# The last two value pieces of a short convolution later, their first taps on VectorE, and a thirteenth seven-product group in the convolution's columns

## The reference, cut to what matters

```python
cqkv = h @ w_in[:, C_CQKV:C_CQKV + 3072]            # 256 x 3072: queries, keys, values, 8 heads each
qkv = silu(causal_depthwise_conv(cqkv, d_conv_w))   # 4 taps over the tokens, each channel by itself
q_c, k_c, v_c = split(qkv, 3)                       # q_c and k_c are then l2-normalized per head
```

## Time and profile before

| what | value |
|---|---|
| median of three runs | 1515.25 us |
| the profiled execution's own time | 1515.99 us |
| its span, first to last instruction | 1514.1 us |
| TensorE clock granted, mean | 1.000 of full speed |
| busy: PE, DVE, ACT, POOL | 1509.8, 1138.6, 821.5, 367.0 us |

### The profile page before, as it was taken

One profiled execution on the slowest core, in us unless ns is written; L12 is line 12 of the kernel. 1 busy time (PEld: TensorE's weight loads), 2 busy tenths in 40 slices (PEclk: granted clock), 3 DMA queues, 4 the chain that ended last, 5 costly groups with the idle time before them and its releaser, 6 DMA issues.

```text
span 1514.1 us, 19057 instructions
## 1 busy us (share of the span) xinstructions
PE 1509.8 (100%) x6900; PEld 1249.9 (83%) x6900; DVE 1138.6 (75%) x1712; ACT 821.5 (54%) x1100; POOL 367.0 (24%) x612
## 2 busy tenths in 40 slices
PE   9999999999999999999999999999999999999999
PEld 7888888888888887888878888888888888888887
DVE  6889899847769855576579676676557789988894
ACT  6766656587533444554545545544345656555563
POOL 9040131330230040126420254344400112000101
PEclk9999999999999999999999999999999999999999
DMA  9876677976788775558765787798875667696867
GB/s 288 283 238 218 198 250 209 254 225 195 223 252 267 235 221 165 158 184 271 248 203 167 231 248 205 241 277 241 236 244 158 216 217 221 205 263 210 237 228 187
DMA packets 209070, 341.47 MB, mean 226 GB/s; under 512 B 53161, under 2 KB 60632, under 8 KB 208720
## 3 DMA queue, kind: packets, MB, share of 16 engines
q1 hardware_dynamic: 184784, 288.66, 61.2%
q0 software_dynamic: 24144, 51.57, 13.1%
q10 hardware_dynamic: 48, 0.02, 0.0%
HBM read 312.81 MB, written 30.83 MB: 227 GB/s over the span
## 4 chain that ended last, share of the span: by engine, by line
PE 98%; DVE 1%; ACT 0%; issue 0%; DMA 0%; DVEq 0%
PE acc L1289 25%; PE acc L1292 25%; PE acc L1291 25%; PE mix L1292 2%; PE mix L1291 2%; PE mix L1289 2%; PE mix L1305 2%; PE mix L1307 2%; PE mix L1306 2%; PE acc L1305 2%; PE acc L1307 2%; PE acc L1306 2%; PE mix L1398 1%; PE mix L1481 1%; PE mix L1470 0%; PE mix L1391 0%
## 5 line engine op out<-in xcount | busy, mean ns | idle before, releaser
L2021 DVE TENSOR_TENSOR w_lo<-w_raw,w_hi 128x1024 fp32r<-128x1024 f32 (+1 forms) x503 | 604.0, 1216 | 252.8 <-ACT w_hi L1626 247.9
L1626 ACT ACTIVATE w_hi<-w_raw 128x1024 fp32r<-128x1024 f32 (+1 forms) x503 | 522.5, 1049 | 371.8 <-PE acc L1292 277.3
L1289 PE MATMUL acc<-w_hi,op_hi 128*128 128x512 f32 (+1 forms) x1628 | 640.4, 393 | 0.3 <-DVE w_lo L2021 0.3
L1292 PE MATMUL acc<-w_hi,op_lo 128*128 128x512 f32 (+1 forms) x1628 | 633.4, 389 | 0.0
L1291 PE MATMUL acc<-w_lo,op_hi 128*128 128x512 f32 (+1 forms) x1628 | 633.3, 389 | 0.0
L1289 PEld LDWEIGHTS acc<-w_hi,op_hi 128*128 128x128 f32 x1628 | 305.7, 188 | 64.7 <-issue 1.3
L1292 PEld LDWEIGHTS acc<-w_hi,op_lo 128*128 128x128 f32 x1628 | 305.6, 188 | 63.8
L1291 PEld LDWEIGHTS acc<-w_lo,op_hi 128*128 128x128 f32 x1628 | 305.8, 188 | 61.9
L993 POOL DMA_DIRECT2D conv_dram<-y x48 | 30.7, 703 | 165.6 <-DVE y L2112 118.4
L1289 PE MATMUL mix<-w_hi,op_hi 128*128 128x512 f32 (+1 forms) x154 | 59.7, 388 | 0.0
L1291 PE MATMUL mix<-w_lo,op_hi 128*128 128x512 f32 (+1 forms) x154 | 59.7, 388 | 0.0
(11 more groups left out here) (566 smaller groups left out, 1798.8 us busy)
## 6 DMA issues: line engine op xcount, KB each, us to landing
w_raw<-in_w_in_dram SPq DMA_DIRECT2D x367, 512.0 KB, 4.5
w_raw<-in_w_out_dram SPq DMA_DIRECT2D x128, 512.0 KB, 4.7
w_raw<-in_w_in_dram SPq DMA_DIRECT2D x16, 384.0 KB, 3.8
w_raw<-in_a_wuq_dram SPq DMA_DIRECT2D x12, 512.0 KB, 5.8
out_dram<-acc POOLq DMA_DIRECT2D x8, 512.0 KB, 7.0
out_dram<-in_x_dram POOLq DMA_DIRECT2D x7, 512.0 KB, 6.3
conv_dram<-y POOLq DMA_DIRECT2D x48, 64.0 KB, 4.0
y<-conv_dram POOLq DMA_DIRECT2D x48, 64.0 KB, 4.3
```

The lines of the kernel that those rows point to most:

```text
L1289: nc.tensor.matmul(o, hi[:, kt, tok], hv[:, i, n0:n1], start=(kt == (kts if late else blk["kts"])[0]), stop=False)
L1292: last_mm = nc.tensor.matmul(o, lo[:, kt, tok], hv[:, i, n0:n1], start=False, stop=(kt == blk["kts"][-1]))
L1626: func(split_ap(w_hi, c), w_raw[:, c % RAW_BUFS, 0:n], ACT.Copy).then_inc(hi_ready, 1)
L2021: vec.tensor_tensor(split_ap(w_lo, c), w_raw[:, c % RAW_BUFS, 0:n], split_ap(w_hi, c).bitcast(F32), ALU.subtract).then_inc(lo_ready, 1)
```

## The change

- `SEVEN`: the second pair of the convolution's columns does tile pair 6 as a group as well (seven groups instead of six; thirteen in the two pairs). `X_S` has 6 too, so its activation sums are made in slots 29 to 31, in `x_more[:, 3]`, `s_more[:, 2]` and `s_more[:, 3]`.
- `CONV_ORDER`: in the first pair the first group is two chunks later (36 and 37); in the second, the sixth group is at chunks 88 and 89, the new one at 92 and 93, before at 86 and 87; each column has nine plain chunks, and the columns end at chunks 94 and 95 (before 88 and 95).
- `CONV_SLOTS`, `PAIR_SLOTS`: other slots for nearly all pieces. Pieces 10 and 11 get their taps in slots 117 and 123 and their silus in 147 and 149.
- `DVE_TAPS`: for pieces 10 and 11 DVE multiplies by the first tap (two instructions more), and ACT does nothing for them but the silu.
- `csq` waits for eight pieces instead of twelve. POOL stores and turns the values after the loads of the triangular systems instead of before the gates' rows, and `vd` is in slots 195 and 197.

```diff
-SEVEN = [[0, 1, 2, 3, 4, 5], [0, 1, 2, 3, 4, 5],
+SEVEN = [[0, 1, 2, 3, 4, 5], [0, 1, 2, 3, 4, 5, 6],
...
-CONV_ORDER = ["12S1111S11S1122S22S22S1222", "12S11S11S11S11S22S12222222"]
-X_S = [0, 1, 2, 3, 4, 5]
-CONV_SLOTS = [(33, 34, 35), (35, 37, 39), (38, 43, 45), (46, 51, 53), (72, 78, 79), (75, 87, 89),
-              (80, 91, 91), (82, 94, 94), (97, 99, 100), (99, 104, 105), (104, 105, 107), (106, 108, 109)]
+CONV_ORDER = ["1211S11S11S1122S22S22S1222", "12S11S11S11S12S2222S22S12"]
+X_S = [0, 1, 2, 3, 4, 5, 6]
+CONV_SLOTS = [(31, 40, 41), (31, 43, 45), (42, 53, 55), (49, 57, 59), (71, 77, 79), (77, 81, 83),
+              (77, 85, 86), (86, 93, 95), (104, 106, 107), (105, 108, 109), (109, 117, 147), (112, 123, 149)]
 CSQ_FROM = 110
-PAIR_SLOTS = [(59, 60, 62, 63), (88, 89, 89, 97)]
+DVE_TAPS = 10
+V_FROM = 195
+PAIR_SLOTS = [(59, 61, 61, 64), (93, 94, 94, 97)]
...
-    weave(g_end + 1, [("vd", 0), ("vd", 1)], 2)
+    weave(V_FROM, [("vd", 0), ("vd", 1)], 2)
...
             def conv(i, use):          # ACT
+                if i >= DVE_TAPS:
+                    return
...
             def csq(i, use):           # ACT
-                act.wait_ge(conv_ready, 12)
+                act.wait_ge(conv_ready, 8)
...
             def conv(i, use):          # DVE
-                dve.wait_ge(conv_y, i + 1)
+                if i < DVE_TAPS:
+                    dve.wait_ge(conv_y, i + 1)
+                else:
+                    dve.wait_ge(conv_turned, i + 1)
+                    for j in range(2):
+                        c = 2 * i + j
+                        row = R_N + (CONV_K - 1) * CH + c
+                        step(vec.tensor_scalar(cT[:, c, :], conv_columns(i, j), par[:, row:row + 1], None, ALU.mult),
+                             but=1 - j)
```

More of the change, by code:

```diff
@@ L1005, in _ @@
                 bring_blocks(conv_stage(j), conv_dram[j % 2], brought[j % 2])
[L1007 to L1016, removed]
             wait_read(pool, "cn", 7)
@@ L1060, in _ @@
                                ).then_inc(lane_left_loaded, 16)
+            pool.wait_ge(conv_ready, 12)
+            for hg in range(2):
+                for i in range(4):
+                    pool.dma_start(v_dram[hg].rearrange("a f j i b -> i a (f j) b")[i],
+                                   v_heads(hg)[32 * i:32 * i + 32].rearrange("p (f b) -> p f b", b=32)
+                                   ).then_inc(v_kept, 16)
+                pool.wait_ge(v_kept, 16 * 4 * (M + hg + 1))
+                for j in range(4):
+                    pool.dma_start(v_heads(hg)[32 * j:32 * j + 32].rearrange("p (f c) -> p f c", c=P),
+                                   v_dram[hg][:, :, j].rearrange("a f i b -> a f (i b)")).then_inc(v_moved[hg], 16)
             pool.wait_ge(v_kept, 16 * 8 * M)
```

## The result

The changed kernel takes 1517.69 us (median of 20 runs, 1515.76 to 1518.79), the kernel before, run beside it, 1515.32 (20 runs). One of these took 3093.89 us, twice the others; the ratio leaves it out. The ratio is 1.0014, 95% interval 1.0007 to 1.002: slower by 2.4 us, of which the interval leaves 1.1 to 3.0. The profiled execution took 1517.55 us with a span of 1515.8, 1.7 more than the span before. The granted clock was 1.000, as before.

What follows compares the result with a forecast made beforehand. PE, busy 1509.8 of 1514.1 us, was taken to set the end, late DVE splits adding directly. Terms -0.68 + 1.0 + 2.1 = +2.4 us on the median of 1515.25 gave 1517.6 us, range 1515.8 to 1519.7.

Steps and rivals of the forecast that it cites:

- The case forecast as likeliest: Waits in chunk 89 and before chunks 127 and 130; 1517.6 us, own range 1516.6 to 1518.6, chance 0.45.
- Term 1: PE's matmuls in the new group: 21 instead of 24, 0.68 us less.
- Term 2: Second pair's columns, chunks 84 to 90: PE waits 1.0 us in chunk 89 for DVE's low part (0.3 to 1.5).
- Term 3: Slot 123, norms and gates: piece 11's taps delay the splits of 127 and 130, +2.1 us (1.9 to 2.4).
- Piece 10 in slot 117: Its taps cost nothing, as following splits had idle time ahead; without that cover, up to 1 us of wait.
- the silus: At 147 and 149, in ACT's half-idle stretch, before anything reads them; no cost counted.
- `csq`: Its wait for eight pieces is met as before; no cost counted.
- the first pair: Its other slots only spread the same pieces; no cost counted, up to 1 us in chunk 34 if cover went.
- `vd`: Moves from a busy to a nearly idle stretch of DVE; gives nothing, as PE had no wait there.
- rival C: Values' stores make weight loads late at chunks 158 to 163: 1519.6 us (1518.6 to 1520.8), chance 0.15.
- Rival D: Columns cost more: a further wait of about 1.3 us behind `evs` in chunks 95 to 98; 1518.9 us, chance 0.13.
- Rivals B and E: B: only slot 123 costs, +1.4, 1516.7 us, chance 0.20. E: only fewer matmuls count, -0.7, 1514.6 us, chance 0.07.

Runs made afterwards that it cites:

- Eased columns: Against the changed kernel: piece 6's taps at 87, 11's at 131, norms three slots later, piece 7's taps at 99, last `evn` at 101; 1514.75 us, again 1515.28.

## Why the prediction was right, and where it was not

The case forecast as likeliest is what happened: waits in the columns and among the gates, each at its chunk and behind the instruction named. 1517.6 us was forecast and 1517.69 measured, but that it is so close is luck: there are two misses of opposite sign, +0.23 in the columns and -0.2 among the gates, and the columns' part differs by 1 us between traces of the same columns.

- **Term 1, -0.68.** Right. Eased columns with and without the group differ by 82.96 - 82.28 = 0.68, and the change is far from paying by it.
- **Term 2, +1.0 in chunk 89.** Right in place, and in size for this trace: chunk 89 took 4.38 us instead of 3.40 (the prediction's own 246.5 - 245.6 gives 0.9 rather than 1.0; 0.84 was the wait and 0.13 the slower matmuls behind it). The queue ran as worked out: reckoned from PE's start on chunk 84, the sums began at +6.69 (forecast +6.55) and the low part was ready at +14.07 (+13.85). One thing I put too low. The lead at chunk 85 was forecast as 0.2 and was 0.05, and chunks 84 and 85 took 2.92 and 2.85 us instead of 2.72: 0.33 that the sum put at nothing. The splits of 84 and 85 were to start from the same place as before; they didn't: chunk 84's lead was 0.64 us, against 0.99 before. The kernel before had 0.13 of its own in these columns (83.09 against the 82.96 without a wait), so the balance is -0.68 + 0.98 + 0.33 - 0.13 = +0.50, measured +0.55. Over the four traces with the changed kernel's columns the waits come to 0.51, 1.14, 1.36 and 1.54 us together, so the term holds as a middle value and the closeness in one trace is chance; its range of 0.3 to 1.5 was needed. Not the new group makes these waits, as the twelve groups show, and the one in chunk 89 goes with piece 6's taps in each of the five kernels that have them at 87. That piece 5's taps in slot 81 make the one at chunk 85 is read from the order in the trace; no run moves them. The prediction named those slots, though it also counted the group's work.
- **Term 3, +2.1 (1.9 to 2.4).** Measured +1.89, just under the lower end: 1.10 in chunk 126, 0.13 in 127, 0.66 in 129. The 1.1 us before 127 is right; of the rest, forecast as 1.0 at 130, 0.66 came, and 0.13 as slower matmuls in 127. The size of the work was right (3.0 to 3.1 us forecast, 3.00 measured). The idle time that it took up was mis-sized. I set off the 0.68 and 0.26 that the trace shows as idle; the split of 130 began 14.20 us after that of 126, where 12.30 + 3.00 - 0.94 = 14.36 was due. The missing 0.16 is overlap. An instruction that follows another without idle time starts some 0.07 to 0.09 before its end, as in 351.73 + 1.22 against 352.87, and one that had to wait doesn't. Where two idle times closed, two such overlaps came back: `ce` 3 begins 2.25 us later against the split of 126 than before, so 0.75 of the 3.00 were taken up where 0.68 was idle, and the split of 128 takes up another 0.35 where 0.26 was.
- **Piece 10 in slot 117, the silus, `csq`, the first pair.** Nothing, as said, and nothing for the activation sums in slots 29 to 31 either: chunks 28 to 64 take 93.84 in all kernels, and 96 to 147 151.15 with piece 11 moved and piece 10 left.
- **`vd`.** Gives nothing: lead at chunk 139 rose from 4.35 to 6.39 us, and PE was never waiting there.
- **The values' stores (rival C).** Nothing. POOL's and ACT's timelines of the changed kernel, for the earlier trace rows:

```profile
432.18 3.14 POOL L1055 DMA_DIRECT2D v_dram<-cT  x4
444.02 0.59 POOL L1060 DMA_DIRECT2D cT<-v_dram  x1 [8.70 <-DMA v_dram<-cT]
```

```profile
441.97 1.06 ACT L1628 ACTIVATE w_hi<-w_raw 128x1024 fp32r<-128x1024 f32 x1 [4.67 <-DMA w_raw<-in_w_in_dram]
```

The late weight load is still there and no later (4.67 us of idle against 5.21); the lead of chunk 158 is 2.56 us (2.03 before). What was later is the stores themselves: POOL waits 8.70 us for its stores to land where it waited 5.15 at 311 us before. The Trainium skill (DMA: Bandwidth & Descriptors, Specifications) says that transfers under 512 B are read, modified and written. The prediction took from this that the weights might come later; this trace shows no such thing for them, and the measurement decides. The stores at their old place in POOL's queue were not tried: POOL would stand there waiting for the silus of slot 149, in front of rows that PE needs sooner.
- **Rival D** was close. The margin at chunks 97 and 98, forecast as 0.9 us, was 0.41 and 0.64, and moving piece 6's taps by two slots used it up at 97.
- **Rivals B and E** fell by the wait in chunk 89 and by slot 123. B is the nearer one: where the lead was longer, in the kernel with piece 11 moved, 0.51 us was left of the columns' waits.

What stays open: why chunks 147 to 490 are longer with twelve groups, where the lead at chunk 75 is lost from trace to trace, and what sets the wait at chunks 506 and 507, which the edits don't touch. Together those two took 5.12 us in before, 5.79 in the changed kernel. DVE's lead there was 0.33 and 0.06 us; stretch 490 to 535 runs from 116.96 to 117.99 over all traces. There is one trace of before, at 117.32, and nine of the eleven others lie above it, so it isn't shown that the change has no part in this.

## What to carry to other kernels

Where one engine is busy all the time and its helper's lead is short, work moved onto the helper costs not by its amount but by what stands behind it in the queue: list the next three deliveries with their lead, and put the new work in the first slot where all of them are longer than it. Moving it by two slots may just hand the wait to the next thin place; check the leads up to where the helper next stands idle. And a saving of 0.68 us can't be seen in runs that scatter by a microsecond or more, but it can in the distances of one engine's instructions. These repeat to 0.01 us where the waits hang on the engines' queues alone (chunks 98 to 147 here), and scattered by 1 us where the lead was short and loads came late (chunks 64 to 96): there, take several traces of the same code before a difference is put down to an edit.

## What was not expected of the hardware

- A matmul behind a wait is shown with 0.50 us instead of 0.39, and the 12 matmuls from it on take 2.85 us instead of 2.72. So each such wait costs 0.13 more than the delay of the first start; it is there at chunks 85, 127 and 130, and at 130 in the kernel before as well.
- DVE's two multiplications of 128x256 by a column take 0.63 us to the start of what follows, 0.31 each; the six taps behind them, one to three columns narrower but adding to what is there, 2.37, 0.40 each.
- Three loads of ACT's tables between neighbours took 1.28 us each and nothing more: 344.18 to the next at 345.91 holds one load and one 8x256 activation of 0.42 us.
- With the same code, the start up to chunk 28 took 87.68 and 86.20 us in two traces of the changed kernel; the difference is more than half of what the change itself costs.
